# Pairing the group norm's row sums, logarithms and exponentials in the scan of a two-block transformer kernel

## The reference, cut to what matters

```python
    y = (y_f + y_b).astype(x.dtype) + xs * d_skip[:, None]
    y = y.reshape(bsz, t, SSM_D_INNER) * jax.nn.silu(z)
    yg = y.astype(jnp.float32).reshape(bsz, t, SSM_GROUPS, SSM_D_INNER // SSM_GROUPS)
    yg = yg * lax.rsqrt(jnp.mean(jnp.square(yg), -1, keepdims=True) + RMS_EPS)
    y = yg.reshape(bsz, t, SSM_D_INNER).astype(x.dtype) * norm_w
    return y @ w_out
```

## Time and profile before

| | |
|---|---|
| median of 3 runs | 2308.41 us (2307.0 to 2309.49) |
| the profiled execution | 2306.67 us, span 2304.8 us |
| PE busy over the span | 2268.8 us, 98% |
| DVE, ACT, POOL busy | 978.4 us (42%), 445.5 us (19%), 74.0 us (3%) |
| TensorE clock granted | 1.00 in every window read |

### The profile page before, as it was taken

One profiled execution on the slowest core, in us unless ns is written; L12 is line 12 of the kernel. 1 busy time (PEld: TensorE's weight loads), 2 busy tenths in 40 slices (PEclk: granted clock), 3 DMA queues, 4 the chain that ended last, 5 costly groups with the idle time before them and its releaser, 6 DMA issues.

```text
span 2304.8 us, 25537 instructions
## 1 busy us (share of the span) xinstructions
PE 2268.8 (98%) x10774; PEld 1367.0 (59%) x10774; DVE 978.4 (42%) x1947; ACT 445.5 (19%) x1013; POOL 74.0 (3%) x130
## 2 busy tenths in 40 slices
PE   8999999999999999999999999999999999999998
PEld 5568547886487459997434333335999643333332
DVE  3567646668576557653211111125764311111122
ACT  3410003257100011220211211101132121111111
POOL 2000000000000000000000000000000000000000
PEclk9999999999999999999999999999999999999999
DMA  7279625454698415246999999994426599999997
GB/s 293 113 304 402 258 78 204 147 183 175 241 409 325 178 60 202 97 177 261 384 428 427 428 427 427 427 419 189 166 96 247 221 409 428 427 427 428 428 428 288
DMA packets 59167, 671.64 MB, mean 291 GB/s; under 512 B 7504, under 2 KB 7792, under 8 KB 18720
## 3 DMA queue, kind: packets, MB, share of 16 engines
q1 hardware_dynamic: 51888, 649.45, 69.1%
q0 software_dynamic: 7152, 20.43, 2.7%
HBM read 666.59 MB, written 3.26 MB: 291 GB/s over the span
## 4 chain that ended last, share of the span: by engine, by line
PE 87%; DMA 9%; DVE 2%; issue 0%; ACT 0%; SPq 0%; POOL 0%; DVEq 0%; POOLq 0%; ACTq 0%
PE ps L101 84%; DMA ring<-in_exp_w 6%; DMA arena<-in_exp_w 2%; DVE arena L114 1%; PE ps L349 1%; DVE arena L117 1%; PE ps L2736 1%; DMA arena<-ssm_rows 1%; DMA ring<-in_attn_w_in 0%; DMA ring<-in_ada_w 0%; PE ps L625 0%; PE ps L1898 0%; DVE X L117 0%; PE ps L1217 0%; ACT arena L106 0%
## 5 line engine op out<-in xcount | busy, mean ns | idle before, releaser
L101 PE MATMUL ps<-arena 128*64 128x512 f32 (+6 forms) x4020 | 952.3, 466 | 13.9 <-DMA arena<-in_exp_w 5.6
L101 PEld LDWEIGHTS ps<-arena 128*128 128x128 f32 (+2 forms) x4020 | 458.7, 167 | 463.8 <-issue 435.3
L101 PE MATMUL ps<-ring,arena 128*64 128x512 f32 (+2 forms) x1720 | 460.6, 584 | 2.1 <-DMA ring<-in_exp_w 2.1
L101 PE MATMUL ps<-XTGB,ring 128*128 128x256 f32 (+1 forms) x2160 | 423.5, 353 | 0.0
L101 PEld LDWEIGHTS ps<-XTGB,ring 128*128 128x128 f32 x2160 | 367.1, 190 | 52.8 <-issue 10.7
L101 PEld LDWEIGHTS ps<-ring,arena 128*64 128x64 f32 (+1 forms) x1720 | 174.4, 150 | 258.9 <-issue 254.7
L122 DVE COPY arena<-ps 128x512 f32<-128x512 f32 (+5 forms) x133 | 63.3, 496 | 417.3 <-PE ps L101 298.5
L121 ACT COPY arena<-ps 128x512 f32<-128x512 f32 (+3 forms) x179 | 81.6, 475 | 678.7 <-PE ps L2736 283.8
L101 PE MATMUL ps<-XTGB,arena 128*64 128x512 f32 (+2 forms) x736 | 200.7, 428 | 0.0
L105 ACT ACTIVATE arena<-ps 128x512 f32<-128x512 f32 (+2 forms) x95 | 51.2, 545 | 677.9 <-PE ps L101 673.0
L101 PE MATMUL ps<-ring,XTGB 128*128 128x512 f32 (+3 forms) x484 | 168.0, 501 | 1.6 <-DMA ring<-in_attn_w_in 1.4
(11 more groups left out here) (150 smaller groups left out, 954.0 us busy)
## 6 DMA issues: line engine op xcount, KB each, us to landing
arena<-in_exp_w SPq DMA_DIRECT2D x90, 2048.0 KB, 26.3
ring<-in_exp_w SPq DMA_DIRECT2D x68, 2048.0 KB, 27.7
ring<-in_mlp_w SPq DMA_DIRECT2D x25, 2048.0 KB, 9.2
ring<-in_ada_w SPq DMA_DIRECT2D x20, 2048.0 KB, 9.7
XTGB<-in_exp_w SPq DMA_DIRECT2D x18, 2048.0 KB, 32.0
ring<-in_ssm_w_in SPq DMA_DIRECT2D x12, 2048.0 KB, 7.8
ring<-in_w_in SPq DMA_DIRECT2D x12, 2048.0 KB, 7.9
ring<-in_gate_w SPq DMA_DIRECT2D x12, 2048.0 KB, 7.9
```

What stands on the lines that cost most here:

```text
L101: return self.e.matmul(o, lhsT=lhsT, rhs=rhs, start=start, stop=stop, skip_group_check=True)
```

## The change

The eight norm groups are handled as four pairs p. PE makes both products with ones of a pair into the two halves of one PSUM bank, in steps 7, 11, 15 and 18, behind `apply` and ahead of that step's `z_chunk` or `so_part`. ACT makes one Ln and one Exp over both groups (128 x 2 x 256), in the same steps, behind `exps`. DVE's `norm_c` comes in steps 8 and 9, 12 and 13, 16 and 17, 19 and 20, one group each, at the end of the step. Nothing else moves.

```diff
-            def norm_b(g):
-                ps = bank(pe, "sn", g)
-                pe.wait_ge(at("ysq", g), at("consts"))
-                pe.then_inc(pe.mm(ps[:, 0:T], C["ones"], xcT[:, 2 * g, :], True, True), ("sn", g))
+            def norm_b(p):
+                ps = bank(pe, "sn", p)
+                for g in (2 * p, 2 * p + 1):
+                    pe.wait_ge(at("ysq", g), at("consts"))
+                    pe.then_inc(pe.mm(ps[:, g % 2 * T:(g % 2 + 1) * T], C["ones"], xcT[:, 2 * g, :], True, True), ("sn", p))
...
-                if i in (SP, SP + 2):
-                    norm_b((i - 4) // 2)
+                if i in (7, 11, 15, 18):
+                    norm_b((i - 6) // 4)
...
-                if 4 <= i < SP and i % 2 == 0:
-                    norm_b((i - 4) // 2)
...
-            def norm_b(g):
-                r = xcT[:, 2 * g, :]
-                act.wait_ge(at("sn", g))
-                k = act.then_inc(act.act(r, ps_of("sn", g)[:, 0:T], ACT.Ln, scale=1.0 / 256, bias=epst),
-                                 ("read", "sn", g))
+            def norm_b(p):
+                r = xcT[:, 4 * p:4 * p + 4, :].rearrange("p (g two) t -> p g two t", two=2)[:, :, 0, :]
+                act.wait_ge(at("sn", p))
+                k = act.then_inc(act.act(r, two(ps_of("sn", p)), ACT.Ln, scale=1.0 / 256, bias=epst),
+                                 ("read", "sn", p))
                 act.wait_ge(k)
-                act.then_inc(act.act(r, r, ACT.Exp, scale=-0.5), ("yr", g))
+                act.then_inc(act.act(r, r, ACT.Exp, scale=-0.5), ("yr", p))
...
-                if i >= 4 and i % 2 == 0 and (i - 4) // 2 < 8:
-                    norm_b((i - 4) // 2)
+                if i in (7, 11, 15, 18):
+                    norm_b((i - 6) // 4)
...
-                v.wait_ge(at("yr", g))
+                v.wait_ge(at("yr", g // 2))
...
-                if i >= 5 and i % 2 == 1 and (i - 5) // 2 < 8:
-                    norm_c((i - 5) // 2)
+                if i in (8, 12, 16, 19):
+                    norm_c((i - 7) // 4 * 2)
+                if i in (9, 13, 17, 20):
+                    norm_c((i - 8) // 4 * 2 + 1)
```

## The result

The change makes the kernel slower: 2315.9 us, median of 9 runs (2311.07 to 2317.93), against 2308.74 us for the kernel before (9 runs, 2307.0 to 2309.92). The ratio is 1.0027, 95% interval 1.0019 to 1.0036. By the medians that is 7.2 us and by the ratio 6.2, where the walk (steps 1 to 9 of the prediction) gave 3.5. The profiled execution took 2317.07 us. The changed kernel's nine runs span 7 us and the nine of the kernel before 3, but that cannot be put down to the change: 20 later runs of the kernel before span 7.2 us (2306.58 to 2313.81).

The account below looks back on a forecast made before the run. PE was taken to bound the kernel, with about 2.7 us of the scan held by E, the matrix `apply` waits for. The terms summed to +3.5 us, on the median 2308.41 giving 2311.9; range 2307 to 2315.5.

Parts of the forecast that it names:

- the walk: Step-by-step reckoning of PE, ACT and DVE over the scan after the change; its terms gave +3.5 us.
- rival C: Scan: decay rows land late and DVE passes on a second wait; slower by over 4.6 us, +7.5, 2315.9; chance 0.22.
- Step 1: ACT: eight table loads fewer and Ln, Exp merged relieve it of about 12.3 us, by itself no kernel time.
- rival D: ACT: each table switch costs more than its load's row, by a pause of about 1.3 us; +5, 2317; chance 0.01.
- Step 3: Apply(3), in step 5: the product of group 0 no longer fills the wait, which becomes 0.93 us; +0.43 us.
- Steps 4, 6 and 8: Waits vanish at apply(5), -0.37 us, apply(9), -0.23, and apply(13), -0.4, with some 0.1 more at apply(14).
- Steps 5 and 7: Apply(7) and apply(11): the pair on ACT delays z_out and Silu, so PE waits 2.7 us at each; +2.1 us each.
- Step 9: End of the norms: last pair takes 4.7 us instead of 3.3, covered before `so_part(3, 0)` with 2.4 us to spare.
- the sum: Scan: 0.43 - 0.37 + 2.1 - 0.23 + 2.1 - 0.4 - 0.1 = +3.5 us; bounds +2.7 to +4.5, +5.5 with late rows.
- The sign given for the first `so_part` behind the last norm: Profile after, end of the scan: this product would come at 591.9 us in place of 588.4.
- Rival A: Scan: ACT's 12 us of relief makes every E early, the 2.7 us of waits vanish; 2305.7; chance 0.13.
- Rival B: Behind the scan: PE's idle places and DMA waits take up the lag; 2308 to 2309; chance 0.14.

## Why the prediction came out as it did

The direction and the mechanism of the waits were right; the size was about half. The forecast said "the same", near its edge, with 0.74, and "slower by over 0.2%" with 0.23; the measured ratio is at 0.27% (0.19 to 0.36), and the median of 2315.9 lies 0.4 above the range's upper end (times 1.0027 on 2308.41, it is 2314.6, inside). That the range came so close is luck: it reached up to 2315.5 for late rows (rival C), and the lag above the sum is the clock's.

- **Step 1**, ACT relieved of 12.3 us: 12.6 on the page. Ln and Exp of 512 columns took 0.69 and 0.63, where 0.68 and 0.63 stood. A load starts where the operation ahead of it ends (523.38 behind exps(7), which ended at 523.37), and the Ln 0.01 us behind the load (524.67), as the rows before had shown. So no pause at a switch of tables is in the chain, and rival D falls.
- **Step 3**, apply(3) +0.43: 508.43 less 503.95 is 4.48, less 3.56 leaves 0.92, for 0.93. Right.
- **Steps 4, 6 and 8**, no waits at apply(5), (9) and (13): right, under 0.1 us each.
- **Steps 5 and 7**, the pivot: apply(7) starts 29.93 us behind z_chunk(8), for 30.0 in the walk; it waits 2.55 us (533.88 less 527.77 and 3.56), apply(11) 2.65, for 2.7 and 2.7. Right, and shown by squares ahead of the Silu (the waits go) and by the unmerged pair (they grow by 2.8 and 3.2).
- **Step 9**, the end: covered, no wait; shown near its limit by the unmerged pair.
- **The failed step is the sum.** It counted PE's waits and took every product behind them at its old duration. The rows had granted 1.00 in every window read, and I carried that over to a kernel whose longest waits are five times as long. The windows read ended at 1000 us; the kernel before has stretches of low clock further on, one of them behind an idle time of 2.75 us (2186.76, granted 0.53 to 2190.00), so its own trace held the price. The missing term: apply(7) and (11) 1.31 and 1.28 us longer, the products behind them 0.22 and 0.35, **3.2 us** in the profiled execution. 3.5 and 3.2 are 6.7 of the 6.9 us of the scan. With idle products in the waits the term goes, and the scan is 3.3 us over the kernel before. The sign given for the first `so_part` behind the last norm missed by it: 591.9 was forecast, and less the 2.0 us ahead of the scan it came at 595.3.
- **Rival C** had the class and, by chance, the time (2315.9), but not the mechanism: it held that late rows would pass the wait on to apply(9) and apply(13), and neither waited. Rival A fell: in the even steps the relief is there in full, and worth nothing (2308.5). Rival B fell: the stretch behind the scan is no shorter after the change (1717.8 and 1718.0 us in its two profiles, 1716.4 before), and the lag of the scan, 6.9 and 5.0 us, is found in the medians, 7.2 and 6.6, and in the ratios, 6.2 and 5.3. Whether the 1.5 us more behind the scan have to do with the change stays open.

## What to carry to other kernels

When work of a side engine is merged, ask into which step of the pipeline the merged piece falls: here the pair went into the very steps whose list on ACT already closed the loop back to PE, and its 3.9 us came on top of a Silu and its table. A wait on PE has two prices, its own length and a slower product behind it where it costs the clock; in the scan before, the longest was 0.45 us of idle time and free of the second, at 1.95 to 2.5 us it cost nothing or about 1.6. If a profile after a change shows the same instruction list with more busy time, look at the granted clock behind each wait, and split the gain in busy time by stretch: here half of it lay outside the part that was changed.

## What the runs showed of the hardware

In the scan, an idle time of PE as short as 2.39 us, in the middle of dense work, was followed by a granted clock of 0.50. Idle times of 1.95 and 2.25 us were not, and 2.49, 2.53, 5.22 and 5.71 were; the products behind such a wait became 1.5 to 1.9 us longer together.

Outside the scan the length of the idle time does not sort the cases. The first row is from the profile with the pairs in the even steps, the other two from the kernel before:

```profile
207.55 1.25 PE L101 MATMUL ps<-arena,c_e 128*3 128x512 f32 x8 [2.03 <-DVE arena L114]
...
1450.07 8.14 PE L101 MATMUL ps<-arena 128*64 128x512 f32 x34 [2.83 <-DMA arena<-in_exp_w]
...
2186.76 9.64 PE L101 MATMUL ps<-arena 128*64 128x512 f32 x34 [2.75 <-DMA arena<-in_exp_w]
```

Behind 2.03 us the granted clock was 0.62 (207.55 to 212.00), behind 2.83 us it stayed at 1.00 (1450.07 to 1453.00), and behind 2.75 us it was 0.53 (2186.76 to 2190.00). The same 34 products took 8.14 us in one case and 9.64 in the other. So the length of the wait alone does not decide: between 2.03 and 2.83 us both outcomes stand in these traces. The Trainium skill, page "TensorE: Matmul & The Clock Gate", Part 1, ties this clock to how busy the engine has been of late and says that the moment at which it changes varies between executions. The traces agree with that much: the two profiles of the changed kernel have two such stretches in the scan in one and one in the other.

Two idle products of 512 columns in each wait made the kernel faster than the change alone: its median lies 4.3 us over that of the kernel before measured beside it, the change's 7.2 and 6.6 us over theirs. The two were not measured side by side, so the 3.6 us of the scan is the firmer number. That is a repair of the symptom: not to wait (2308.5) is better.
